# Four source tiles, one head multiply, earlier LoRA loads and six paced groups in a two-block kernel

## The reference

```
def first_block(x, ...):
    xn = rms_norm(h, ln_attn_pre)
    proj = xn @ w_in                          # 1024 x 3328
    y_rwkv = rwkv7_mix(proj[..., :1792], ...)  # 8 heads of 64, LoRA decay, iclr and gate
    o = diff_attention(dq, dk, dv, lam, slopes)   # 4 heads of 2 x 64, causal, ALiBi
    o = rms_norm(o, diff_subln, eps=SUBLN_EPS) * (1.0 - lam_init)
    h = h + rms_norm(concat([y_rwkv, o]) @ w_out, ln_attn_post)
    hn = rms_norm(h, ln_ffn_pre)
    u = causal_dwconv(hn @ w_up, conv_w, conv_b)      # 1024 -> 2 x 2816
    f = (gelu(gate) * val) @ w_down
    return h + rms_norm(f, ln_ffn_post)

def second_block(x, ...):
    proj = rms_norm_2(x, norm1) @ w_in
    log_f = log_sigmoid(fa + forget_bias)     # 8 forget gates a token
    o_a = forgetting_attention(qa, ka, va, log_f)   # causal, bias from cumsum(log_f)
    o_b = chunk_band_attention(qc, kc, vc, rel_bias)
    x = x + (g_a * (o_a @ w_branch_a) + g_b * (o_b @ w_branch_b)) @ w_out
    x = x + square(relu(rms_norm_2(x, norm2) @ w_up)) @ w_down    # 1024 -> 4096
    return rms_norm_2(x, final_norm)
```

## Time and profile before

| | |
|---|---|
| time, three runs | 3179.58, 3185.03 and 3189.38 us, median 3185.03 |
| the profiled execution | 3189.02 us, its span 3187.3 |
| PE busy | 3037.9 us, 95% of the span |
| DVE, ACT, POOL busy | 48%, 30%, 20% |
| mean granted clock of PE | 0.986 |
| DMA | 292.80 MB, mean 92 GB/s |

### The profile page before, as it was taken

One profiled execution on the slowest core, in us unless ns is written; L12 is line 12 of the kernel. 1 busy time (PEld: TensorE's weight loads), 2 busy tenths in 40 slices (PEclk: granted clock), 3 DMA queues, 4 the chain that ended last, 5 costly groups with the idle time before them and its releaser, 6 DMA issues.

```text
span 3187.3 us, 48853 instructions
## 1 busy us (share of the span) xinstructions
PE 3037.9 (95%) x20514; PEld 2439.7 (77%) x20514; DVE 1526.2 (48%) x1887; ACT 968.5 (30%) x1438; POOL 634.7 (20%) x276
## 2 busy tenths in 40 slices
PE   8999988889899999999899999999899999999998
PEld 6877767778688888888588867666688888888887
DVE  3156668741744444445711145556454444444445
ACT  3155545532421222213321133434332211111112
POOL 3311121222321222212043300000022221122211
PEclk9999999999999999999999999999899999999999
DMA  5533330021411111111353533354544411111111
GB/s 193 160 113 93 119 109 25 25 69 53 159 47 47 39 59 50 49 40 40 123 152 124 186 109 116 120 149 125 202 133 133 130 47 33 53 53 53 46 33 66
DMA packets 235008, 292.80 MB, mean 92 GB/s; under 512 B 10057, under 2 KB 182226, under 8 KB 234842
## 3 DMA queue, kind: packets, MB, share of 16 engines
q1 hardware_dynamic: 219866, 243.22, 24.9%
q10 hardware_dynamic: 14976, 47.19, 3.8%
HBM read 209.86 MB, written 80.51 MB: 91 GB/s over the span
## 4 chain that ended last, share of the span: by engine, by line
PE 85%; DVE 6%; issue 5%; ACT 2%; DMA 1%; POOL 0%; DVEq 0%; ACTq 0%; SPq 0%; POOLq 0%
PE ps L368 62%; PE ps L1385 4%; PE ps L1955 4%; PE ps L542 4%; PE ps L2025 2%; PE ps L2006 2%; PE ps L1983 1%; PE ps L1448 1%; PE ps L1986 1%; DVE y L2459 1%; DVE cb L2563 1%; DMA residual<-src 0%; PE ps L1426 0%; DVE stage L2169 0%; DVE pbuf L2149 0%
## 5 line engine op out<-in xcount | busy, mean ns | idle before, releaser
L345 POOL TENSOR_TENSOR wl<-wraw,wh 128x1024 fp32r<-128x1024 f32 x151 | 369.2, 2445 | 1693.6 <-ACT wh L340 1693.6
L368 PE MATMUL ps<-xh,wh 128*128 128x512 f32 x2192 | 682.8, 393 | 10.0 <-DVE xl L441 2.8
L368 PE MATMUL ps<-xl,wh 128*128 128x512 f32 x2192 | 678.9, 391 | 0.0
L368 PE MATMUL ps<-xh,wl 128*128 128x512 f32 x2192 | 678.0, 391 | 0.0
L368 PEld LDWEIGHTS ps<-xh,wh 128*128 128x128 f32 x2192 | 409.5, 188 | 108.3 <-DVE xl L441 8.9
L368 PEld LDWEIGHTS ps<-xh,wl 128*128 128x128 f32 x2192 | 413.7, 189 | 87.0
L368 PEld LDWEIGHTS ps<-xl,wh 128*128 128x128 f32 x2192 | 413.4, 189 | 86.7
L340 ACT ACTIVATE wh<-wraw 128x1024 fp32r<-128x1024 f32 x167 | 176.9, 1059 | 924.6 <-PE ps L368 862.6
L2459 DVE TENSOR_TENSOR y<-ps,y 128x1024 f32<-128x1024 f32 x208 | 253.2, 1222 | 241.6 <-PE ps L368 241.4
L2367 POOL TENSOR_TENSOR dl<-draw,dh 128x2048 fp32r<-128x2048 f32 x25 | 119.1, 4764 | 521.0 <-ACT dh L2363 521.0
L2504 DVE SCALAR_TENSOR_TENSOR cb<-ub,cols,cb 128x1024 f32<-128x1024 f32 x88 | 129.4, 1470 | 61.2 <-ACT cb L2541 56.1
(11 more groups left out here) (345 smaller groups left out, 4421.9 us busy)
## 6 DMA issues: line engine op xcount, KB each, us to landing
wraw<-in_w_up SPq DMA_DIRECT2D x76, 512.0 KB, 3.9
wraw<-in_w_in SPq DMA_DIRECT2D x67, 512.0 KB, 4.1
draw<-in_w_down SPq DMA_DIRECT2D x27, 1024.0 KB, 5.0
residual<-src ACTq DMA_DIRECT2D x32, 512.0 KB, 5.0
proj<-stage SPq DMA_DIRECT2D x30, 512.0 KB, 2.9
qk_hi<-hs ACTq DMA_DIRECT2D x24, 512.0 KB, 2.8
qk_lo<-ls SPq DMA_DIRECT2D x24, 512.0 KB, 2.9
kh<-qk_hi SPq DMA_DIRECT2D x48, 256.0 KB, 7.0
```

The costliest lines, as they stand in the source:

```text
L345: nc.gpsimd.tensor_tensor(wl[:, s, :, :], wraw[:, s, :, :], wh[:, s, :, :].bitcast(F32), ALU.subtract).then_inc(w_lo, 1)
L368: mm = nc.tensor.matmul(ps[:, bank + h, :], w, x[:, h * HALF:(h + 1) * HALF], start=start and k == 0, stop=stop and k == 2)
```

## The change

Seven edits in one:

1. First norm: four source tiles instead of two (`src_first`); a copy waits for the users of the tile four back, and ACT's store waits for the store before it on the same semaphore.
2. `normed` is one multiply of 128x1024 with a broadcast operand, and stands behind `combine(2)` instead of in front of `inverse(2)`. `osq1` is held twice.
3. "decayed" of RWKV tile 0 goes ahead of the last input unit's evacuation; PE waits for that evacuation at block 4.
4. SP loads the LoRA weights of RWKV tile 1 before it waits for the stage stores.
5. `paced_units`: six groups of the second unit stand among the tiles instead of four; one group stands before the spread, one behind it.
6. Post-norm 1: ACT splits the weights of unit `U_QKV2 + 2` ahead of the forget gates, and DVE's first forget-gate instruction goes ahead of two waits for stores.
7. `down_bank_free`: with `behind=True` (the last chunk of each feed-forward) the first down product waits only for the adds up to the one before the last; the second product now has a wait of its own in every chunk.

```diff
@@ -139,6 +139,7 @@
         src = at("src", 184, [P, 2, T])
+        src_first = [src[:, 0, :], src[:, 1, :], at("src2", 157, [P, T])[:, :], at("src3", 161, [P, T])[:, :]]
         sq = at("sq", 192, [P, 2, T])
...
@@ -430,15 +431,15 @@
-            kt, s = r % KT, r % 2
+            kt, tile = r % KT, src_first[r % 4] if r < KT else src[:, r % 2, :]
             act.wait_ge(ready[0], ready[1])
-            nc.scalar.activation(xh[:, kt, :], src[:, s, :], ACT.Identity, scale=col(gain, kt)).then_inc(x_hi, 1)
-            square_act(act, q, src[:, s, :])
+            nc.scalar.activation(xh[:, kt, :], tile, ACT.Identity, scale=col(gain, kt)).then_inc(x_hi, 1)
+            square_act(act, q, tile)
         def prep_dve(dve, r, q, gain, sums=False):
-            kt, s = r % KT, r % 2
+            kt, tile = r % KT, src_first[r % 4] if r < KT else src[:, r % 2, :]
             dve.wait_ge(x_hi, r + 1)
-            nc.vector.scalar_tensor_tensor(out=xl[:, kt, :], in0=src[:, s, :], scalar=col(gain, kt),
+            nc.vector.scalar_tensor_tensor(out=xl[:, kt, :], in0=tile, scalar=col(gain, kt),
                                            in1=xh[:, kt, :].bitcast(F32), op0=ALU.mult, op1=ALU.subtract)\
@@ -474,17 +475,15 @@
                 mm = products(0, kt)
-                if kt == 3:
+                if kt == 1:
                     pe.wait_ge(w_lo, n + 2)
                     pe.wait_ge(evac_done, n)
-                if 3 <= kt < KT - 1:
-                    products(1, kt - 3)
+                if 1 <= kt < KT - 1:
+                    products(1, kt - 1)
             mm.then_inc(mm_done, 1)
-            for kt in range(4, KT):
-                if kt == 6:
-                    spread_pe(pe, k)
-                mm = products(1, kt)
-            mm.then_inc(mm_done, 1)
+            products(1, 6)
+            spread_pe(pe, k)
+            products(1, 7).then_inc(mm_done, 1)
@@ -583,8 +582,8 @@
                     rw_dve.wait(pe, "G1", j - 1)
-                else:
-                    pe.wait_ge(evac_done, IN_TILES)
+            elif b == 4 and j == 0:
+                pe.wait_ge(evac_done, IN_TILES)
             g, i = b // 4, b % 4
...
@@ -1428,7 +1428,7 @@
             def turn_output(b, h):
-                d1_dve.wait(pe, f"on{b}{TT - 1}", 0)
+                d1_dve.wait(pe, f"on{b}", 0)
                 bank_free([(d1_act, f"ot{b}{h}"), (d1_dve, f"lo{b}{h}")])
...
@@ -1632,11 +1632,10 @@
                 d1_act.wait(dve, f"root{b}", 0)
-                d1_dve.done(nc.vector.reciprocal(osq1[:, :], osq1[:, :]), f"rr{b}")
+                d1_dve.done(nc.vector.reciprocal(osq1[b % 2][:, :], osq1[b % 2][:, :]), f"rr{b}")
                 d1_dve.wait(dve, f"rr{b}", 0)
-                for i in range(TT):
-                    part = osb1[b % 2][:, i, :]
-                    d1_dve.done(nc.vector.tensor_scalar(part, part, osq1[:, i:i + 1], None, ALU.mult), f"on{b}{i}")
+                part = osb1[b % 2][:, :, :]
+                d1_dve.done(tt(part, part, osq1[b % 2][:, :].unsqueeze(2).broadcast_to([P, TT, P]), ALU.mult), f"on{b}")
@@ -1693,8 +1692,6 @@
                 for n in range(TT):
-                    if n == 1 and b:
-                        normed(b - 1)
                     if n + 1 < TT:
@@ -1710,6 +1707,8 @@
                         combine(b, n + 1)
+                    if n == 1 and b:
+                        normed(b - 1)
                     shift()
@@ -1729,8 +1728,8 @@
             prepare_dve(dve, 0, "mixed")
+            prepare_dve(dve, 0, "decayed")
             evac(13)
-            prepare_dve(dve, 0, "decayed")
             scores_dve(dve, 0)
@@ -2377,29 +2376,34 @@
-        def down_products(pe, steps, c, d, par, hi=None, lo=None):
+        def down_bank_free(pe, d, m, behind):
+            if m > 1:
+                pe.wait_ge(down_added, KT * d + m)
+            else:
+                pe.wait_ge(down_added, KT * d + (m if behind else 1))
+        def down_products(pe, steps, c, d, par, hi=None, lo=None, behind=False):
             hi, lo = hi or dh, lo or dl
...
-                if m != 1:
-                    pe.wait_ge(down_added, KT * d + max(m - 1, 0) + 1)
+                down_bank_free(pe, d, m, behind)
                 for kt in range(2):
...
-        def token_products(pe, steps, c, d, par, hi=None, lo=None):
+        def token_products(pe, steps, c, d, par, hi=None, lo=None, behind=False):
             hi, lo = hi or dh, lo or dl
...
-                if m != 1:
-                    pe.wait_ge(down_added, KT * d + max(m - 1, 0) + 1)
+                down_bank_free(pe, d, m, behind)
                 t = slice(m * P, (m + 1) * P)
@@ -2643,11 +2647,13 @@
             d1_program_sp(sp)
+            lora_weights(1)
             for s in range(2):
...
             for j in range(1, RWKV_TILES):
-                lora_weights(j)
+                if j >= 2:
+                    lora_weights(j)
                 rwkv_loads(j)
@@ -2887,7 +2893,9 @@
                 prep_act(act, kt, kt, "ln_attn_pre", (src_ready, kt + 1))
-                act.dma_start(residual[kt], src[:, s, :]).then_inc(src_stored[s], 16)
+                if kt >= 2:
+                    act.wait_ge(src_stored[s], 16 * (kt // 2))
+                act.dma_start(residual[kt], src_first[kt % 4]).then_inc(src_stored[s], 16)
             stat_root_act(act, 0)
@@ -2938,6 +2946,7 @@
             rstd_copy_act(act, 4)
+            split_hi(act, U_QKV2 + 2, U_QKV2 % 2)
             act.wait_ge(fa_dve, 2)
@@ -2949,7 +2958,8 @@
                 k = u % 2
-                split_hi(act, U_QKV2 + 2 + u, (U_QKV2 + k) % 2)
+                if u:
+                    split_hi(act, U_QKV2 + 2 + u, (U_QKV2 + k) % 2)
                 act.wait_ge(evac_done, U_QKV2 + 1 + u)
@@ -3046,7 +3056,7 @@
             down_products(pe, ff1_dve, DOWN1 - 2, DOWN1 - 2, 1)
-            down_products(pe, ff1_dve, DOWN1 - 1, DOWN1 - 1, 0, dh_last, dl_last)
+            down_products(pe, ff1_dve, DOWN1 - 1, DOWN1 - 1, 0, dh_last, dl_last, behind=True)
             post_sums_pe(pe, 24)
...
@@ -3135,16 +3145,18 @@
                     dve.wait_ge(xt_done, kt + 1)
-                    if kt >= 2:
-                        dve.wait_ge(x_lo, kt - 1)
-                        dve.wait_ge(x_sq, kt - 1)
-                        dve.wait_ge(src_stored[s], 16 * (kt // 2))
-                    nc.vector.tensor_copy(src[:, s, :], bank2(1 + 2 * s)).then_inc(src_ready, 1)
+                    if kt >= 4:
+                        dve.wait_ge(x_lo, kt - 3)
+                        dve.wait_ge(x_sq, kt - 3)
+                        dve.wait_ge(src_stored[s], 16 * (kt // 2 - 1))
+                    nc.vector.tensor_copy(src_first[kt % 4], bank2(1 + 2 * s)).then_inc(src_ready, 1)
                 if kt:
...
             dve.wait_ge(rstd_copied, 1)
+            for s in range(2):
+                dve.wait_ge(src_stored[s], 16 * 4)
@@ -3184,11 +3196,10 @@
+            nc.vector.tensor_tensor(fa[:, :], ps[0:FOX_HEADS, 0:2, :].rearrange("p a n -> p (a n)"),
+                                    rstd[0:FOX_HEADS, :], ALU.mult).then_inc(evac_done, 1)
             for s in range(2):
                 dve.wait_ge(src_stored[s], 16 * 12)
-            nc.vector.tensor_tensor(fa[:, :], ps[0:FOX_HEADS, 0:2, :].rearrange("p a n -> p (a n)"),
-                                    rstd[0:FOX_HEADS, :], ALU.mult).then_inc(evac_done, 1)
             dve.wait_ge(fa_loaded, 16)
```

More of the change, by code:

```diff
@@ L264, in build_program @@
         weight1 = at("weight1", 102.75, [P, TT])
-        osq1 = at("osq1", 102.875, [P, TT])
+        osq1 = [at("osq1_0", 102.875, [P, TT]), at("osq1_1", 102.90625, [P, TT])]
         hs1 = at("hs1", 165, [P, 2, T], F32R)
@@ L1297, in d1_names @@
                     act += [f"root{b - 1}", f"ot{b - 1}0", f"ot{b - 1}1"]
-                    dve += [f"rr{b - 1}"] + [f"on{b - 1}{i}" for i in range(TT)] + [f"lo{b - 1}0", f"lo{b - 1}1"]
+                    dve += [f"rr{b - 1}", f"on{b - 1}", f"lo{b - 1}0", f"lo{b - 1}1"]
                     pe += [f"to{b - 1}0", f"to{b - 1}1"]
@@ L1308, in d1_names @@
                         act.append(f"root{b - 1}")
-                        dve += [f"rr{b - 1}"] + [f"on{b - 1}{i}" for i in range(TT)]
                     if n + 1 < TT:
@@ L1327, in d1_names @@
                         dve.append(f"pb{b}{n + 1}")
+                    if n == 1 and b:
+                        dve += [f"rr{b - 1}", f"on{b - 1}"]
                     if more:
@@ L1520, in square @@
                     d1_act.wait(act, f"sq{b}{n - 1}" if n else f"sq{b - 1}{TT - 1}", 0)
-                d1_act.done(fn(sq_out[:, :], osb1[b % 2][:, n, :], ACT.Square, accum_out=osq1[:, n:n + 1]), f"sq{b}{n}")
+                d1_act.done(fn(sq_out[:, :], osb1[b % 2][:, n, :], ACT.Square, accum_out=osq1[b % 2][:, n:n + 1]), f"sq{b}{n}")
             def root(b):
                 d1_act.wait(act, f"sq{b}{TT - 1}", 0)
```

(4 more changed lines are left out.)

## The result

The changed kernel takes 3165.44 us (median of six runs, 3160.26 to 3167.0), the one before beside it 3184.04 (six runs, 3176.75 to 3189.38): a ratio of 0.9942, 95% interval 0.9927 to 0.9957. In two further sets of runs it was 0.9934 (0.9921 to 0.9947) and 0.9939 (0.9925 to 0.9953). The forecast was 3163, between 3155 and 3173, and faster. One run of the kernel before in the second set, of 3349.95 us at a granted clock of 0.873, was in a slower state and is left out of every comparison.

A forecast was written before the change was run, and what follows sets the result against it. The prediction took the kernel as matmul-bound (PE 85% of the chain), with only PE's pauses and low-clock stretches to win. Its terms summed to −23.3 us, 3161.7 from the median 3185.0; it said 3163, range 3155 to 3173.

The forecast's parts named there:

- A: First norm, four source tiles: PE's pause goes (−2.3) and the low clock behind it (−1.7), −4.0 us in all.
- rival 1: The clock is not given back and only the pauses go: 3171 to 3172 us; chance 0.20.
- B: Attention heads 1 to 3, one later multiply: pauses 2.07 to about 0.25 (−5.4), clock behind them −4.2 us.
- C: RWKV, copies ahead of the last input unit's evacuation: PE's 4.76 us wait for bt falls to 3.3, −1.4 us.
- D: RWKV tile 1, LoRA weights issued earlier: wait of 1.3 to 1.7 left (−2.6), clock −1.85, sum −4.4 us.
- E1: Post-norm 0, paced units: gain 0, PE's wait for wl grows to 3.7 and costs clock, +1.9 us.
- E2: Post-norm 1 and forget gates: earlier weight split starts unit +2 sooner, then unit +3's weights limit; −3.0 us.
- Rival 2: More than counted: E1's longer pause costs no clock and LoRA weights land in time, 3159 to 3160; chance 0.11.
- F: Last chunk of either feed-forward, down_bank_free: two pauses of 1.41 us go, −2.8 us.
- Rival 3: Feed-forward loops: the added wait at the second group is not free, 3197 us at 1.3 each; chance 0.03.
- The sum: Whole kernel: all parts together −23.3 us, giving 3165.7 from the profiled execution or 3161.7 from the median.
- Rival 4: The change does little: pauses move to the next need, B, D and E2 at half, 3170 us; chance 0.06.

The follow-up runs named there:

- part B alone: The kernel before with only the head normalised by one broadcast multiply, behind combine(2): 0.9974 of the kernel before, 3175.67 us.
- zero_by_tile: The changed kernel, but POOL zeroes each tile of y as soon as the norm is done with it: 0.9933 of the kernel before, 3161.79 us.
- Both experiments: The changed kernel with the old pacing in post-norm 0 alone, 3163.17 us; and the changed kernel with y zeroed tile by tile, 3161.79 us.
- rel_in_parts: The changed kernel, but the store rel_d is issued in four parts behind later weight loads: 0.993 of the kernel before, 3163.75 us.

## Why the prediction was right

*A, the first norm: right in its pause, partly wrong in its clock.* The pause of 2.33 went. The 1.7 us of low clock were in one profile of before and not in the other, nor in that of part B alone, where the pause was still there. So A is 2 to 4 us by execution; 2.3 was the lower bound. For this term rival 1 was right.

*B: right, term by term.* Pauses 1.81 less each (5.4); the clock's 4.2 came to 4.6 (head 2 3.07 less 0, head 3 12.45 − 9.12 − 1.8 = 1.5). That a low stretch of the attention belongs to the pause, which rival 1 disputed, is borne out: two profiles of before with 2.07 us pauses have both stretches, eleven profiles of eight kernels with shorter pauses have none. But head 1's pause, 2.04 us in one profile and 2.07 in the other, had none in either, and 2.07 is the length that cost clock at heads 2 and 3. So the prediction's contrast of 2.04 with 2.07 was no contrast of length: the same length costs clock in one place and not in another, and what decides stays open. That the two stretches go with the pauses' shortening is shown, the reason is not.

*C: right.* 3.4 left of 4.8; −1.4.

*D: its wait a little too long, its clock wrong.* The wait left was 1.5, 0.3 and 1.3, and 0.5, 1.2, 1.1 and 0.2 in the four other kernels with the load behind the store (mean 0.9, forecast 1.3 to 1.7). It was 4.0, 3.6 and 1.8 in the three profiles with the old order. The small ones of either order (0.2, 0.3, 0.5 and 1.8) are those in which PE ran at half clock for longer before it and so came later to the same weights: the wait is shorter, the time isn't. The 1.85 us of clock were one execution's; for this term too rival 1 was right.

Moving the load ahead of the store takes the wait away, so the store in front does hold the weights back. In the changed profile it landed at 439.75 + 4.7 = 444.4, the weights (both loads count on one semaphore) at 444.73, and PE started at 444.77. SP had needed 2.09 us to issue the second load (0.60 before), but this isn't the cause: in `zero_by_tile` SP needed 0.73, and the weights still landed 0.31 us behind the store, as in six of the seven profiles with this order. In the seventh, the multiply merged but not moved, the store landed early, at 446.61, and the weights 2.04 us later, so there something else was last. That the weights never land before the store fits the rule that the prediction cites from the Trainium skill (DMA: Bandwidth & Descriptors, on queues, rings and completion order); whether their data or only their count is late no trace here tells.

```profile
440.11 0.48 SPq L2631 DMA_DIRECT2D lora_w<-in_w_decay_up  x1
440.64 2.09 SPq L2632 DMA_DIRECT2D lora_w<-in_w_iclr_up  x1
```

and in `zero_by_tile`:

```profile
440.38 0.73 SPq L2632 DMA_DIRECT2D lora_w<-in_w_iclr_up  x1
```

*E1: right in mechanism and sign.* The wait of 3.7 at `wl` behind the memsets and the low clock behind it; +2.2 instead of +1.9. Both experiments agree on the cause. Rival 2 (this pause costs no clock) falls.

*E2: the step that failed.* −3.0 was forecast, −0.5 came. (With four more kernels that have the same post-norm 1 the stage is 83.03 to 84.80 us in seven profiles, mean 83.9, against 85.24, 84.49 and 85.39 with the old one: −1.2, still less than half.) The limit was named rightly, unit +3's weights, but the step took their landing, 1609.22, as a fixed time. Their load is issued behind `rel_d`, and that behind POOL's work on `rel`, so it moves with the norm: in all seven the stage ends 24.5 us after POOL's op on `rel`, early or late. In the changed profile POOL finished `rel` at 1573.89, where 1590.12 less the 18.2 us that the kernel was ahead by then would be 1571.9: two us late, because the norm ended 1.4 later against its start (the sums at 1526.83 and the spread behind them ran at half clock, 0.9, and a tile slipped by 0.5), and because the op on `rel` took 2.11 instead of 1.57 (in all ten profiles with the new code against all three with the old; why isn't known). The same 18.3 us of landing then passed on those two. `rel_in_parts` shows what the part could have won: 82.15 is 2.9 below the mean of before. The clock of this part, 1.7 us behind the `stage` pause, is in two of the three old profiles and in none of the ten new ones.

*F: right.* Forecast 1.4 each, 1.67 came: the pause and the slower first two matmuls behind it. The added wait costs nothing: the loops without the last chunks are 660.0 us against 660.3, 770.6 against 770.5. Rival 3 falls.

*The sum.* −23.3 was applied to one execution of before whose span was 3.1 us above the second profile's and whose time was 4 above the median, and which held 3.6 us of low clock in A and D that isn't always there. The three pairs of medians give −18.6, −19.8 and −19.2, so the sum was some 4 us too large: E2's missing 2 us or so, and the clock of A and D. PE's busy time says the same: by the means it fell by 5.4 us, and B's 4.6 nearly fill that. The forecast of 3163 lay 1.3 above the sum's 3161.7, for which the prediction gives no reason; that it came within 2.5 us of all three medians is partly luck. Rival 4 (the pauses move to the next need) falls for B, whose 1.81 us a head came in full, and is what happened in E2.

## To carry to other kernels

A pause in a busy stream of matmuls is priced with the clock behind it, but only after further profiles have shown that stretch again: here 4.6 us were the kernel's, 3.6 one execution's, and 1.7 came in two profiles of three. A wait that shrinks because the engine came later has won nothing: look at when the awaited thing was ready. When PE is given work earlier, look for what the next unit needs and who makes it; if that engine has a block of its own behind the same event (the eight memsets), nothing is won and the longer pause costs clock. A time at which a DMA landed isn't a fixed bound: find what it was issued behind.

## What was not expected of the hardware

- At heads 2 and 3 a pause of 2.07 us of PE was followed by half clock in four of four cases (2 profiles), and at head 1 pauses of 2.04 and 2.07 us in none of two. Behind pauses of 1.63 us there was none in three cases (1 profile), behind the pause of 3.7 us at `wl` there was in six of six.
- Behind a store of 768 KB from eight partitions, copied 32 times, a load of 512 KB on the same queue took 18.2 to 18.3 us to land in all ten profiles that have the store in one piece, instead of 3.8 to 4.0. With the store in four parts behind later loads no weight load up to 1727 us took more than 4.8 in that run.
- Eight memsets on POOL beside VectorE's work took 0.95 us each instead of 0.90, and the norm kept its period of 3.70 us.
- A multiply of 128x1024 with a broadcast 128x8 operand takes 1.22 us, eight of 128x128 with a scalar per partition 1.66.
